# Three weight and activation sums of the first gate/up round, made by accumulating DMAs instead of VectorE

## The reference

```
h = rms_norm(x, g_ffn_pre)                                # 512 x 2048
ff = (silu(h @ w_gate) * (h @ w_up)) @ w_down             # 2048 -> 5632 -> 2048
x = x + rms_norm(ff, g_ffn_post)
```

## Time and profile before

| | |
|---|---|
| three runs | 1922.96 us median (1921.97 to 1924.96) |
| profiled execution | 1920.78 us, its span 1918.9 us |
| TensorE busy | 1881.9 us (98%) |
| VectorE busy | 1515.7 us (79%) |
| ScalarE busy | 915.4 us (48%) |
| GpSimd busy | 53.4 us (3%) |
| granted TensorE clock | 0.998 of full speed |

### The profile page before, as it was taken

The page is one execution under the profiler, slowest core; times in us unless marked ns, Lnnn a source line. Parts: engine busy times, 40 slices in busy tenths (PEclk is TensorE's granted clock), DMA queues, the critical chain, the costliest instruction groups (busy, mean ns, idle before and its releaser), DMA issues.

```text
span 1918.9 us, 22133 instructions
## 1 busy us (share of the span) xinstructions
PE 1881.9 (98%) x8730; PEld 1559.5 (81%) x8730; DVE 1515.7 (79%) x1606; ACT 915.4 (48%) x1220; POOL 53.4 (3%) x41
## 2 busy tenths in 40 slices
PE   8999999999999999999999999999999999999998
PEld 6888788888887778888888888888888788888886
DVE  5763496676466988888988888888889888888888
ACT  6331394455464645454554545545455733333332
POOL 1210040000000000000000000000000000000000
PEclk9999999999999999999999999999999999999999
DMA  8434201116675245263462643725436866547563
GB/s 245 115 95 114 87 24 61 61 67 246 237 263 197 80 141 183 92 230 113 140 218 78 209 136 117 248 83 175 163 107 230 307 251 236 205 163 268 212 228 131
DMA packets 205251, 314.28 MB, mean 164 GB/s; under 512 B 7555, under 2 KB 142812, under 8 KB 199260
## 3 DMA queue, kind: packets, MB, share of 16 engines
q1 hardware_dynamic: 202112, 306.21, 46.5%
q10 hardware_dynamic: 3036, 6.66, 1.1%
HBM read 263.01 MB, written 52.98 MB: 165 GB/s over the span
## 4 chain that ended last, share of the span: by engine, by line
PE 61%; DVE 3%; issue 1%; DMA 1%; ACT 0%; DVEq 0%; ACTq 0%
PE pair L2584 13%; PE pair L2586 13%; PE pair L2585 13%; PE pair L2633 6%; PE pair L2635 6%; PE pair L2634 6%; PE pair L2595 1%; PE pair L2654 1%; PE pair L2653 1%; PE pair L2652 1%; DVE unit_lo L1866 1%; DMA w_b<-in_w_down 1%; DVE ring_lo L2111 0%; DVE xf_lo L1860 0%; DVE w2a L1891 0%
## 5 line engine op out<-in xcount | busy, mean ns | idle before, releaser
L2584 PE MATMUL pair<-unit_hi,xf_hi 128*128 128x512 f32 x1224 | 481.7, 394 | 7.9 <-DVE unit_lo L1866 7.9
L2586 PE MATMUL pair<-unit_hi,xf_lo 128*128 128x512 f32 x1224 | 477.0, 390 | 0.0
L2585 PE MATMUL pair<-unit_lo,xf_hi 128*128 128x512 f32 x1224 | 476.4, 389 | 0.0
L2584 PEld LDWEIGHTS pair<-unit_hi,xf_hi 128*128 128x128 f32 x1224 | 229.8, 188 | 58.3 <-issue 7.3
L2586 PEld LDWEIGHTS pair<-unit_hi,xf_lo 128*128 128x128 f32 x1224 | 229.7, 188 | 48.6
L2585 PEld LDWEIGHTS pair<-unit_lo,xf_hi 128*128 128x128 f32 x1224 | 230.0, 188 | 46.3
L459 DVE TENSOR_TENSOR wlo<-raw,whi 128x2048 fp32r<-128x2048 f32 (+2 forms) x62 | 131.0, 2119 | 94.5 <-ACT whi L452 94.4
L2633 PE MATMUL pair<-ring_hi,hfs 128*128 128x512 f32 x480 | 187.4, 390 | 1.4 <-ACT ht L1314 0.8
L452 ACT ACTIVATE whi<-raw 128x2048 fp32r<-128x2048 f32 (+2 forms) x62 | 109.6, 1775 | 163.8 <-PE pair L712 155.9
L2634 PE MATMUL pair<-ring_lo,hfs 128*128 128x512 f32 x480 | 186.8, 389 | 0.0
L2635 PE MATMUL pair<-ring_hi,hfs 128*128 128x512 f32 x480 | 186.8, 389 | 0.0
(11 more groups left out here) (377 smaller groups left out, 3407.1 us busy)
## 6 DMA issues: line engine op xcount, KB each, us to landing
w_b<-in_w_down SPq DMA_DIRECT2D x40, 1024.0 KB, 5.1
h_forms<-h_stage SPq DMA_DIRECT2D x71, 512.0 KB, 4.9
raw<-in_w_o SPq DMA_DIRECT2D x32, 1024.0 KB, 5.1
hfs<-h_forms SPq DMA_DIRECT2D x30, 1024.0 KB, 8.3
raw<-in_w_in SPq DMA_DIRECT2D x18, 1024.0 KB, 5.8
w1a<-in_w_gate SPq DMA_DIRECT2D x16, 512.0 KB, 3.6
w1a<-in_w_up SPq DMA_DIRECT2D x16, 512.0 KB, 5.4
w1b<-in_w_gate SPq DMA_DIRECT2D x16, 512.0 KB, 3.7
```

What stands on the lines that cost most here:

```text
L2584: nc.tensor.matmul(dst, a[0], w[0], start=(at, k) == (0, 0), stop=False)
L2585: nc.tensor.matmul(dst, a[0], w[1], start=False, stop=False)
L2586: last = nc.tensor.matmul(dst, a[1], w[0], start=False, stop=(at, k) == (3, 1))
```

## The change

In the first round only, three things that VectorE made are made by DMAs that GpSimd issues and that add to what is in their destination:

- S4 (form 4 of A, in two halves): x_a12 gets x_s2 added. For this VectorE makes the negative of S2 (S3 - A22), so that the addition gives A12 - S2.
- T3, in two halves of 128x2048: B11 gets the slot of T2 added. VectorE makes the negative of T2 (T1 - B22), so this gives B11 - T2, the negative of T3. One DMA for a half, 1 MB.
- T4, in two halves: the slot of T2, once product 2 has been split, gets B21 added straight from DRAM, four DMAs of 128x2x256 for a half. This gives B21 - T2 = T4. The second load of B21 by SyncE is gone.

ScalarE copies the high half of form 2 with a scale of -1, and VectorE makes its low half as -x_s2 - hi (a SCALAR_TENSOR_TENSOR), so that form 2 is S2 itself. Products 2 and 3 of the first round have negative weights and are subtracted instead of added. The low half of form 2 now waits for S4's DMA, `s4_in[j]`. From the second round on everything is as it was.

```diff
+            def add_t2_to_b11(half):
+                s1, s2, _ = slots(0)
+                pool.wait_ge(u_lo, unit_no(0, 0, 2 * half + 1) + 1)
+                pool.wait_ge(g_sum, half + 3)
+                nc.gpsimd.dma_start(w_slot[s1][half][:, :, :], w_slot[s2][half][:, :, :],
+                                    accum_op=ALU.add).then_inc(t3_in[half], 16)
+
+            def add_b21_to_t2(half):
+                place = w_slot[slots(0)[1]][half]
+                pool.wait_ge(u_lo, unit_no(0, 2, 2 * half + 1) + 1)
+                pool.wait_ge(t3_in[half], 16)
+                for w_v, c0 in ((wg_v, 0), (wu_v, 256)):
+                    for k in (0, 2):
+                        nc.gpsimd.dma_start(place[:, k:k + 2, c0:c0 + 256],
+                                            w_v[:, 1, 4 * half + k:4 * half + k + 2, 0:256],
+                                            accum_op=ALU.add).then_inc(t4_in[half], 16)
+
+            def add_s2_to_a12(j):
+                pool.wait_ge(x_lo, x_count(5, 0))
+                pool.wait_ge(x_sum, (S2_0, S2_1)[j])
+                nc.gpsimd.dma_start(x_raw(4, j), x_raw(2, j), accum_op=ALU.add).then_inc(s4_in[j], 16)
+
+            add_s2_to_a12(0)
+            add_t2_to_b11(0)
+            add_s2_to_a12(1)
+            add_t2_to_b11(1)
+            for half in range(2):
+                add_b21_to_t2(half)
...
                             if f_ == 3:
-                                load(b, "b21", v // 2)
+                                if b:
+                                    load(b, "b21", v // 2)
...
                                 if f_ == (5 if b else 6):
-                                    sp_.wait_ge(g_sum, 8 * b + 7 + v // 2)
+                                    if b:
+                                        sp_.wait_ge(g_sum, sums_before(b) + 7 + v // 2)
                                     load(b + 1, "b12", v // 2)
...
+                elif f_ == 4:
+                    act.wait_ge(s4_in[j], 16)
                 else:
                     act.wait_ge(x_sum, SUMS_DONE[f_, j])
-                nc.scalar.activation(xf_hi[f_][:, 4 * j:4 * j + 4, :], x_raw(f_, j), ACT.Copy).then_inc(x_hi, 1)
+                hi = xf_hi[f_][:, 4 * j:4 * j + 4, :]
+                if f_ == 2:
+                    nc.scalar.activation(hi, x_raw(f_, j), ACT.Copy, scale=-1.0).then_inc(x_hi, 1)
+                else:
+                    nc.scalar.activation(hi, x_raw(f_, j), ACT.Copy).then_inc(x_hi, 1)
...
                 elif f_ in (2, 3, 6):
-                    act.wait_ge(g_sum, 8 * b + {2: 2, 3: 4, 6: 6}[f_] + v // 2 + 1)
+                    if b == 0 and f_ != 2:
+                        act.wait_ge((t3_in if f_ == 3 else t4_in)[v // 2], 16 if f_ == 3 else 64)
+                    else:
+                        act.wait_ge(g_sum, sums_before(b) + {2: 2, 3: 4, 6: 6}[f_] + v // 2 + 1)
...
-                    last = nc.vector.tensor_tensor(s2, a22, s3, ALU.subtract)
-                else:
-                    dve.wait_ge(x_sum, (S2_0, S2_1)[j])
-                    last = nc.vector.tensor_tensor(a12, a12, s2, ALU.subtract)
+                    last = nc.vector.tensor_tensor(s2, s3, a22, ALU.subtract)
...
                     if f_ != 1:
-                        dve.wait_ge(x_sum, (S4_0, S4_1)[j])
-                nc.vector.tensor_tensor(dst, raw_form, hi, ALU.subtract).then_inc(x_lo, 1)
+                        dve.wait_ge(x_sum, (S2_0, S2_1)[j])
+                if f_ == 2:
+                    dve.wait_ge(s4_in[j], 16)
+                    nc.vector.scalar_tensor_tensor(out=dst, in0=raw_form, scalar=-1.0, in1=hi, op0=ALU.mult,
+                                                   op1=ALU.subtract).then_inc(x_lo, 1)
+                else:
+                    nc.vector.tensor_tensor(dst, raw_form, hi, ALU.subtract).then_inc(x_lo, 1)
...
-                    nc.vector.tensor_tensor(s2, s3, t1, ALU.subtract).then_inc(g_sum, 1)
+                    a, c = (s3, t1) if b else (t1, s3)
+                    nc.vector.tensor_tensor(s2, a, c, ALU.subtract).then_inc(g_sum, 1)
...
-                nc.vector.tensor_tensor(dst, a, product_bank(b, f_)[:, :, :], ALU.add).then_inc(c_added, 1)
+                turned = b == 0 and f_ in (2, 3)
+                nc.vector.tensor_tensor(dst, a, product_bank(b, f_)[:, :, :],
+                                        ALU.subtract if turned else ALU.add).then_inc(c_added, 1)
...
-            x_sum_of(S4_0)
...
-            x_sum_of(S4_1)
...
-            weight_sum(0, 3, 0)
...
-            weight_sum(0, 3, 1)
...
-            weight_sum(0, 6, 0)
...
-            weight_sum(0, 6, 1)
```

More of the change, by code:

```diff
@@ L317, in build @@
         g_sum = sem("g_sum")
+        s4_in = [sem(f"s4_in{i}") for i in range(2)]
+        t3_in = [sem(f"t3_in{i}") for i in range(2)]
+        t4_in = [sem(f"t4_in{i}") for i in range(2)]
         u_hi = sem("u_hi")
@@ L528, in x_raw @@
             return {1: x_a21, 2: x_s2, 3: x_s3, 4: x_a12, 6: x_a22}[f_][:, 4 * j:4 * j + 4, :]
-        S3_0, S1_0, S2_0, S3_1, S1_1, S4_0, S2_1, S4_1 = range(1, 9)
-        SUMS_DONE = {(1, 0): S1_0, (1, 1): S1_1, (2, 0): S2_0, (2, 1): S2_1, (3, 0): S3_0, (3, 1): S3_1,
-                     (4, 0): S4_0, (4, 1): S4_1}
+        S3_0, S1_0, S2_0, S3_1, S1_1, S2_1 = range(1, 7)
+        SUMS_DONE = {(1, 0): S1_0, (1, 1): S1_1, (2, 0): S2_0, (2, 1): S2_1, (3, 0): S3_0, (3, 1): S3_1}
         def x_count(f_, j):
@@ L644, in unit_place, with sums_before @@
             return unit_hi[u % 3], unit_lo[u % 3]
+        def sums_before(b):
+            return 8 * b - 4 if b else 0
         def t1_count(b, half):
-            return (2, 1)[half] if b == 0 else 8 * b + half + 1
+            return (2, 1)[half] if b == 0 else sums_before(b) + half + 1
         def product_bank(b, f_):
@@ L668, in build @@
             s1_, s2_, s3_ = slots(b_)
-            for what_, slot_ in ((("b11", s1_), ("b21 first", s3_), ("b12", s2_), ("b22", s3_), ("b21", s1_)) if b_ == 0
+            for what_, slot_ in ((("b11", s1_), ("b21 first", s3_), ("b12", s2_), ("b22", s3_)) if b_ == 0
                                  else (("b11", s1_), ("b12", s2_), ("b22", s3_), ("b21", s1_))):
@@ L1414, in form_hi @@
                     act.wait_ge(u_lo, 28 * ROUNDS - 4)
-                    act.wait_ge(g_sum, 8 * ROUNDS)
+                    act.wait_ge(g_sum, sums_before(ROUNDS))
                 elif n == 14:
@@ L1832, in x_sum_of @@
             def x_sum_of(which):
-                j = {S3_0: 0, S1_0: 0, S2_0: 0, S4_0: 0}.get(which, 1)
-                a11, a12, a21, a22 = a11_raw(j), x_raw(4, j), x_raw(1, j), x_raw(6, j)
+                j = int(which > S2_0)
+                a11, a21, a22 = a11_raw(j), x_raw(1, j), x_raw(6, j)
                 s2, s3 = x_raw(2, j), x_raw(3, j)
@@ L1841, in x_sum_of @@
                     last = nc.vector.tensor_tensor(a21, a21, a22, ALU.add)
-                elif which in (S2_0, S2_1):
+                else:
                     dve.wait_ge(x_sum, (S3_0, S3_1)[j])
-                    last = nc.vector.tensor_tensor(s2, a22, s3, ALU.subtract)
-                else:
-                    dve.wait_ge(x_sum, (S2_0, S2_1)[j])
-                    last = nc.vector.tensor_tensor(a12, a12, s2, ALU.subtract)
+                    last = nc.vector.tensor_tensor(s2, s3, a22, ALU.subtract)
                 last.then_inc(x_sum, 1)
@@ L1881, in weight_sum @@
                         dve.wait_ge(used, Q_FFN)
-                    nc.vector.tensor_tensor(s2, s3, t1, ALU.subtract).then_inc(g_sum, 1)
+                    a, c = (s3, t1) if b else (t1, s3)
+                    nc.vector.tensor_tensor(s2, a, c, ALU.subtract).then_inc(g_sum, 1)
                 elif form == 3:
-                    dve.wait_ge(g_sum, 8 * b + half + 3)
+                    dve.wait_ge(g_sum, sums_before(b) + half + 3)
                     dve.wait_ge(u_lo, unit_no(b, 0, 2 * half + 1) + 1)
@@ L1888, in weight_sum @@
                     dve.wait_ge(*loaded(b, "b21", half))
-                    dve.wait_ge(g_sum, 8 * b + half + 5)
+                    dve.wait_ge(g_sum, sums_before(b) + half + 5)
                     dve.wait_ge(u_lo, unit_no(b, 2, 2 * half + 1) + 1)
```

## The result

The change makes the kernel slower: 1930.04 us (median of six runs, 1929.23 to 1931.46) against 1923.07 us for the kernel before on the same chip, ratio 1.0035, 95% interval 1.0024 to 1.0046. The forecast was 1918.0 us and "faster"; the time lies outside its range of 1915.0 to 1925.0 us.

What follows compares the result with a forecast made beforehand. VectorE was taken to bound the first round's stretch from 636.4 to 691.0 us. Of 8.5 us lost, 1.6 and 1.9 stay, so 5.0 us less: 1918.0 us against a median of 1922.96, range 1915.0 to 1925.0.

Steps and rivals of the forecast that it cites:

- 8.5 us lost before, VectorE the bound: First round, 636.4 to 691.0 us: TensorE's 46.1 us of work takes 54.6 because VectorE is late; 8.5 us is the most to gain.
- 1.6 us of late starts stay: First round, units 10 to 12: VectorE's low halves still come late, by 0.1, 0.7 and 0.6 us; 1.6 us stay lost.
- S4's half 1 lands at 648.9 and 1.9 us are lost at unit 13: First round: S4's half 1, queued behind T3's half 0, holds up VectorE's low half of form S2; unit 13 loses 1.9 us.
- 6.0 us per MB and 1.2 us fixed: Price of the first round's accumulating transfers: 6.0 us per MB for two operands read, 1.2 us fixed from a store's landing.
- The estimate of 4.8 us per MB: Alternative transfer price from the skill's pages: S4's half 1 lands at 647.1 us, 0.1 us lost, 6.8 us gained in all.
- T4 follows with 1 MB a half ... about 661 and 667 us at 6 us per MB: First round: T4's halves land at about 661 and 667 us, ahead of units 24 and 26, wanted about 674 and 680.
- The first: Rival, chance 0.25: accumulation costs at most 5 us per MB, S4's half 1 lands by 647.4; 6.7 us less, 1916.3 us.
- The third: Rival, chance 0.18: transfer engines add far slower than they copy; at 15 us per MB 20 us slower, 1943 us.
- The second: Rival, chance 0.2: first round's transfers start late or run at a third of a copy's rate, gain given back, 1922.5 us.
- The clock: TensorE's granted clock was taken as 1.00 (2.4 GHz) before, in and after the first-round stretch, so it gives nothing back.

## Why the prediction was wrong

- **8.5 us lost before, VectorE the bound.** Right: 8.7 us by the gaps, and with VectorE relieved nothing is lost before units 14 to 25.
- **1.6 us of late starts stay.** Right: 0.2 + 0.6 + 0.8.
- **S4's half 1 lands at 648.9 and 1.9 us are lost at unit 13.** The mechanism and the place were right, the size 1.2 us short: it landed at 650.1, and 3.1 us were lost. T2's half 0 ended at 638.68 and the transfer was issued 0.6 us later, at 639.27, which I had left to the range. From there the 1.5 MB took 10.9 us; I had 1.2 + 9.0.
- **6.0 us per MB and 1.2 us fixed.** Both terms were off, in opposite directions. In one queue the transfers within SBUF land one behind the other: T3's half 0 at 647.7, S4's half 1 (0.5 MB) 2.5 us later, T3's half 1 (1 MB) another 4.9 us later; with S4 first the two halves of T3 land 5.0 us apart. So the data cost 4.9 to 5.0 us per MB. The row of S4's half 1 in the changed kernel, from the list for 641 to 642 us:

```profile
x_a<-x_s POOLq DMA_DIRECT2D x1, 512.0 KB, 8.6
```

What is fixed is then 3.4 us for T3's half 0 (8.4 less 4.9 to 5.0) and 2.1 us for S4's half 1 where it goes first (4.6 less 2.5), not 1.2, which I had from a store alone; the two load rows beside it would have given 2.1 (3.6 less 1.5). Against 3.4 us, the fixed part was 2.2 us too small and the data 1.6 us too dear, and 0.6 us went by before the issue; that the landing was only 1.2 us off is partly luck. The estimate of 4.8 us per MB from the Trainium skill's pages (Collectives: The Full Stack, on the two source reads, and DMA: Bandwidth & Descriptors) is borne out by the 4.9 to 5.0 here; the landing at 647.1 that I worked out with it is not, for the fixed part. (The section "Specifications" of the second page has 435 GB/s and not 436, which leaves the estimate at 4.8.)
- **"T4 follows with 1 MB a half ... about 661 and 667 us at 6 us per MB."** This is the step that failed. I priced eight transfers as two of 1 MB, and let only their data count, without a landing for each. They were issued one at a time, 18 us for a MB: half 0 was there at 671, within its time, half 1 at 695.3, where ScalarE wanted it at 681.7 (695.35 less 13.61). With the larger ring, the kernel takes 1919.35 us, inside the range, in place of 1930.04.
- **Rivals.** None had it. The first had the price of the data right (at most 5 us per MB), and not the landing that it drew from it. The third named the sign and the place ("T4 half 1 late too") with the wrong cause: a slow addition, which was to make S4 late by far more. The second had GpSimd's descriptor writing as what makes transfers late, but beside a busy VectorE; GpSimd issued each in 0.85 to 1.22 us, at its time, until the ring was full. One term of that rival was too small: a wait to 645.1 at 640.87 moves unit 11 by 4.2 us, not 3.6, which leaves its total about where it was.
- **The clock.** I took it as given, since it was 1.00 throughout. A gap on TensorE cost more than its length where the clock fell with it: here 2.2 us on top of 9.0.
- **What stays open.** The kernel with the larger ring should by its gaps (4.7 us lost) be 4.0 us faster than before and was 2.7 (0.9982, interval 0.9973 to 0.9991, which reaches to 5.2 us). In its profiled execution the round begins 1.6 us later than in that of the kernel before (608.81 against 607.24 us). The executions scatter by as much ahead of the round: the kernel with S4 first begins it 2.2 us late, the one with half of T4 on top, whose code up to there is the same, not at all. A wait of TensorE of 1.0 us for `c_p` between 705 and 800 us stands in its trace and not in that of before. Whether the medians hold these too is not shown. What a descriptor takes of the ring was not measured; only that 1024 bytes had room for one piece of 256 rows or three of 128 at a time, and 2048 for three of 256.

## What to carry to other kernels

Before work is moved to DMAs that GpSimd issues, count the rows of each and ask how many transfers their descriptor ring holds: if it is one, the cost is the whole time from issue to landing for each transfer (here 4.6 us for 256 KB), not the data's time, and the due time of the last one decides. Price each transfer up to its landing, from the event that lets it be issued, and put the short one with the early due time ahead of the long one that nobody awaits. Moving only as much as the ring carries in time, with S4 put first, beat the change as it was made by 14.7 us (1930.04 to 1915.30 us, on two chips whose kernels before differ by 0.3 us); some 3.7 of these are the order, by the runs with and without it.

## What the runs showed of the hardware that was not expected

- The ring's serialising: 4.6 us from issue to issue of 256 rows at 1024 bytes, against three pieces within 1.5 us at 2048 (654.50 to 655.95).
- An accumulation within SBUF moves at 4.9 to 5.0 us per MB behind another in the queue (T3 and S4 here), with 2.1 to 3.4 us fixed.
- Transfer queues slow each other: T4's pieces of 256 KB went from 4.2 to 5.9 and 7.5 us where SyncE's loads ran beside them (4.5 to 4.7 us throughout with all but one pair of the loads held back), and SyncE's load of `w1a<-in_w_up` at 674 us (512 KB) took 6.3 us in the changed kernel, against 4.5 for the same load before.
- The granted clock fell to 0.50 after idle times of TensorE of 9.0 us (ten steps of 0.43 us), 6.8 us (eight, with T4 in sixteen pieces), 5.7 us (ten) and 2.85 us (eight), all before unit 26, but not after those of 2.8 to 3.1 us before unit 13. In the windows of the kernel with T4 within SBUF and of the one with the loads held back:

```profile
688.30:692.30 4.00, 3.96 (x11) 3.16 (x12) 4.00 (x4) 2.72 (x6) 0.00 (x0) 0.60 1.10 348
```

```profile
654.00:658.00 4.00, 3.96 (x17) 3.30 (x18) 3.39 (x3) 0.92 (x1) 1.22 (x1) 1.00 0.49 72
```

The first follows 2.85 us of idle time before unit 26 with 0.60 of the clock as the mean and 11 matmuls, the second follows 3.1 us before unit 13 with 1.00 and 17. What sets the two apart was not tried.
